# Attention scores from a stacked high-and-low split of queries and keys in place of one fp32 product

## What is computed

```python
def forgetting_attention(q, k, v, f_logit, b_f):
    log_f = jax.nn.log_sigmoid(f_logit.astype(jnp.float32) + b_f.astype(jnp.float32))
    F = jnp.cumsum(log_f, axis=1).transpose(0, 2, 1)
    ...
    def block(args):
        qi, Fi, i = args
        q_pos = i * Q_BLOCK + jnp.arange(Q_BLOCK)
        logits = jnp.einsum('bhqd,bhkd->bhqk', qi, k).astype(jnp.float32) * scale
        logits = logits + (Fi[..., :, None] - F[..., None, :])
        logits = jnp.where(q_pos[:, None] >= k_pos[None, :], logits, -jnp.inf)
        p = jax.nn.softmax(logits, axis=-1)
        return jnp.einsum('bhqk,bhkd->bhqd', p.astype(v.dtype), v)
    ...
```

## Time and profile before

| | |
|---|---|
| median of 3 runs | 2919.59 us |
| lowest, highest | 2916.76, 2920.18 us |
| profiled execution, span | 2917.4 us |
| TensorE busy | 2802.4 us (96%) |
| TensorE weight loads | 2225.7 us (76%) |
| DVE busy | 1768.7 us (61%) |
| ACT busy | 1035.1 us (35%) |
| POOL busy | 26.2 us (1%) |
| mean granted TensorE clock | 0.980 |
| attention stage | about 470.6 to 757 us |

### The profile page before, as it was taken

How to read it: one execution, slowest core, us unless ns; L and a number is a source line. 1 busy time by engine, 2 the same in 40 slices (tenths; PEclk the granted TensorE clock), 3 DMA queues, 4 the chain that set the end, 5 groups by cost and what they waited for, 6 DMA issues and landing times.

```text
span 2917.4 us, 35290 instructions
## 1 busy us (share of the span) xinstructions
PE 2802.4 (96%) x12481; PEld 2225.7 (76%) x12481; DVE 1768.7 (61%) x2713; ACT 1035.1 (35%) x1629; POOL 26.2 (1%) x44
## 2 busy tenths in 40 slices
PE   6999999999999999999999999999999899999996
PEld 3468887777788866788877778787788688888885
DVE  6855675555588757444465747473967776335444
ACT  3032222444332355432243534443422622234224
POOL 0000000000000000000000000000000000000000
PEclk9999999999999989999999999999999999999998
DMA  9966552222356646465522222234566365332331
GB/s 346 350 208 223 187 180 89 73 75 78 128 191 214 223 142 232 156 211 196 183 78 89 89 80 96 72 93 167 198 223 219 101 215 187 98 94 98 127 123 58
DMA packets 240190, 451.26 MB, mean 155 GB/s; under 512 B 23849, under 2 KB 45819, under 8 KB 235437
## 3 DMA queue, kind: packets, MB, share of 16 engines
q1 hardware_dynamic: 237236, 440.80, 45.7%
q0 software_dynamic: 2304, 8.39, 0.8%
q10 hardware_dynamic: 504, 0.17, 0.0%
HBM read 422.01 MB, written 27.30 MB: 154 GB/s over the span
## 4 chain that ended last, share of the span: by engine, by line
PE 74%; issue 13%; DVE 5%; ACT 3%; DVEq 2%; DMA 1%; ACTq 1%; SPq 1%; POOLq 0%; POOL 0%
PE ps L1311 18%; PE ps L1314 18%; PE ps L1317 18%; PE ps L1536 3%; PE ps L1764 2%; PE ps L1324 1%; PE ps L1330 1%; PE ps L1327 1%; PE ps L1268 1%; PE ps L1281 1%; PE ps L1795 1%; PE ps L1798 1%; PE ps L1286 1%; PE ps L1283 1%; PE ps L1681 1%
## 5 line engine op out<-in xcount | busy, mean ns | idle before, releaser
L1311 PE MATMUL ps<-op_hi,w_hi 128*128 128x512 f32 (+2 forms) x2800 | 783.9, 399 | 21.1 <-ACT op_hi L919 7.5
L1821 DVE TENSOR_TENSOR w_lo<-w_raw,w_hi 128x512 fp32r<-128x512 f32 (+2 forms) x672 | 440.9, 662 | 598.0 <-ACT w_hi L681 330.0
L1317 PE MATMUL ps<-op_hi,w_lo 128*128 128x512 f32 (+2 forms) x2800 | 757.1, 390 | 4.0 <-DVE w_lo L1821 4.0
L1314 PE MATMUL ps<-op_lo,w_hi 128*128 128x512 f32 (+2 forms) x2800 | 760.3, 391 | 0.0
L1311 PEld LDWEIGHTS ps<-op_hi,w_hi 128*128 128x128 f32 (+1 forms) x2800 | 520.7, 190 | 140.6 <-issue 26.0
L1317 PEld LDWEIGHTS ps<-op_hi,w_lo 128*128 128x128 f32 (+1 forms) x2800 | 528.7, 189 | 116.2 <-DVE w_lo L1821 5.2
L1314 PEld LDWEIGHTS ps<-op_lo,w_hi 128*128 128x128 f32 (+1 forms) x2800 | 530.0, 189 | 112.8 <-issue 0.3
L681 ACT ACTIVATE w_hi<-w_raw 128x512 fp32r<-128x512 f32 (+2 forms) x416 | 242.6, 592 | 619.5 <-PE ps L1317 451.9
L1844 DVE SCALAR_TENSOR_TENSOR acc<-a_raw,vec,acc 128x512 f32<-128x512 f32 x525 | 381.7, 746 | 15.7 <-DMA a_raw<-in_w_ada 12.8
L706 ACT ACTIVATE w_hi<-w_raw 128x512 fp32r<-128x512 f32 x288 | 181.7, 632 | 588.4 <-PE ps L1317 456.2
L2524 DVE TENSOR_TENSOR w_lo<-w_raw,w_hi 128x512 fp32r<-128x512 f32 x128 | 83.6, 686 | 65.1 <-ACT w_hi L1181 59.8
(11 more groups left out here) (274 smaller groups left out, 2456.8 us busy)
## 6 DMA issues: line engine op xcount, KB each, us to landing
a_raw<-in_w_ada SPq DMA_DIRECT2D x216, 512.0 KB, 4.0
w_raw<-in_w_in_e SPq DMA_DIRECT2D x160, 512.0 KB, 4.7
w_raw<-in_w_in SPq DMA_DIRECT2D x96, 512.0 KB, 4.8
arena<-in_w_ada SPq DMA_DIRECT2D x72, 512.0 KB, 6.8
w_raw<-in_w_in_o SPq DMA_DIRECT2D x64, 512.0 KB, 4.4
w_raw<-in_w_out SPq DMA_DIRECT2D x32, 512.0 KB, 4.8
w_raw<-in_w_out_e SPq DMA_DIRECT2D x32, 512.0 KB, 5.0
w_raw<-in_w_out_o SPq DMA_DIRECT2D x32, 512.0 KB, 3.8
```

What stands on the lines that cost most here:

```text
L1311: mm(ps[0:m, bank + j, 0:tok], hi[:, cols], B.op_hi[:, k, 0:tok], start=first, stop=False)
L1314: mm(ps[0:m, bank + j, 0:tok], hi[:, j * P:j * P + m], B.op_lo[:, k, 0:tok], start=False, stop=False)
L1317: last = mm(ps[0:m, bank + j, 0:tok], lo[:, j * P:j * P + m], B.op_hi[:, k, 0:tok], start=False, stop=last_t)
L1821: V.tensor_tensor(B.w_lo[:, c % RING, 0:width], B.w_raw[:, c // 2 % RAW, c % 2, 0:width], B.w_hi[:, c % RING, 0:width].bitcast(f32), ALU.s ...
```

## The change

Queries q and keys k are split into an fp32r high part and a low part (the rest). A buffer `stage` of three tiles of 128 x 512 is made for each head, with two buffers in turn (one in the place of `B.acc`, one in the arena). With own the 64 rows of the head and other the other 64:

- tile ST_Q: own rows the high part of q, other rows its low part
- tile ST_HIGH: the high part of k, in own and other rows alike
- tile ST_LOW: the low part of k, in own and other rows alike

The score is now two fp32r products into one bank, ST_Q by ST_HIGH and ST_Q by ST_LOW: all 128 rows are used, and (q high + q low) by (k high + k low) comes out.

POOL makes the own rows: two copies with a change of type, and one subtraction. ACT copies the high part of k to the other rows (`stage_high`, in the unit of 256 of the head before, ahead of its exponential). DVE makes the low part of q and k in the other rows (`stage_low`, two subtractions, in the unit of 256 of the head before, behind its `w_lo` tile). Head 0 is made before the stage, behind `part_summed`.

```diff
+def stage_low(B, dve, h):
+    dve.wait_ge(B.sem("stage_high"), h + 1)
+    own, other = head_rows(h)
+    q, k = head_source(B, h)
+    for part, x, high in ((ST_Q, q, ST_Q), (ST_LOW, k, ST_HIGH)):
+        last = B.nc.vector.tensor_tensor(B.stage[h % 2][other, part, :], x,
+                                         B.stage[h % 2][own, high, :].bitcast(mybir.dt.float32),
+                                         mybir.AluOpType.subtract)
+    last.then_inc(B.sem("stage_other_low"), 1)
...
 # pool_program
-    pool.wait_ge(sem("mixing"), HEADS_A)
     for h in range(HEADS_B):
-        if h < 2:
-            nc.gpsimd.memset(queries[others, h, :], 0.0)
-        if h >= 2:
+        if h == 0:
+            pool.wait_ge(sem("part_summed"), o)
+        elif h == 1:
+            pool.wait_ge(sem("mixing"), HEADS_A)
+            pool.wait_ge(sem("mixed"), HEADS_A)
+        else:
             pool.wait_ge(sem("scores"), 4 * (h - 1) + 1)
-        nc.gpsimd.tensor_copy(queries[rows, h % 2, :], B.Y[rows, 8 + h // 2, :])
-        nc.gpsimd.drain().then_inc(sem("queries_in"), 1)
+        nc.gpsimd.tensor_copy(stage[own, ST_Q, :], q)
+        nc.gpsimd.tensor_copy(stage[own, ST_HIGH, :], k)
+        nc.gpsimd.drain().then_inc(sem("stage_high"), 1)
+        nc.gpsimd.tensor_tensor(stage[own, ST_LOW, :], k, stage[own, ST_HIGH, :].bitcast(mybir.dt.float32),
+                                mybir.AluOpType.subtract)
+        nc.gpsimd.drain().then_inc(sem("stage_own_low"), 1)
...
 # attention_scalar
+        Act(B.stage[h % 2][other, ST_HIGH, :], k, ACT.Copy).then_inc(sem("stage_other_high"), 1)
...
+        if u % 4 == STAGE_AT and u // 4 + 1 < HEADS_B:
+            stage_high(u // 4 + 1)
...
 # attention_tensor
-            pe.wait_ge(sem("queries_in"), s // 4 + 1)
-            mm(ps[:, 4 + s % 2, 0:P * (b + 1)], at(AT_QST, 2, S)[:, half, b * P:(b + 1) * P],
-               keys[:, pair, 0:P * (b + 1)], start=True, stop=True).then_inc(sem("scores"), 1)
+            if b == 0:
+                pe.wait_ge(sem("stage_other_high"), s // 4 + 1)
+                pe.wait_ge(sem("stage_own_low"), s // 4 + 1)
+                pe.wait_ge(sem("stage_other_low"), s // 4 + 1)
+            queries = B.stage[half][:, ST_Q, b * P:(b + 1) * P]
+            high, low = (B.stage[half][:, k, 0:P * (b + 1)] for k in (ST_HIGH, ST_LOW))
+            mm(ps[:, 4 + s % 2, 0:P * (b + 1)], queries, high, start=True, stop=False)
+            mm(ps[:, 4 + s % 2, 0:P * (b + 1)], queries, low, start=False, stop=True).then_inc(sem("scores"), 1)
...
 # attention_vector, behind low_to(min(u + 3, UNITS + 4)) and ahead of gated
+        if u % 4 == STAGE_AT and u // 4 + 1 < HEADS_B:
+            stage_low(B, dve, u // 4 + 1)
```

More of the change, by code:

```diff
@@ L192 @@
 AT_VA, AT_K, AT_V, AT_WST, AT_BS, AT_F, AT_FQ = 2048, 6144, 10240, 14336, 15360, 16384, 16896
-AT_NEGF, AT_LOGIT, AT_PT, AT_OTOK, AT_QST, AT_KST = 2048, 3072, 4096, 5120, 14336, 15360
+AT_NEGF, AT_LOGIT, AT_PT, AT_OTOK, AT_STAGE = 2048, 3072, 4096, 5120, 14336
+ST_Q, ST_HIGH, ST_LOW = 0, 1, 2
 AT_XRES, AT_SQ, AT_RSTD, AT_SUM, AT_QSUM = 2048, 4096, 8192, 12544, 13568
@@ L225, in __init__ @@
         self.acc = sb("acc", [P, 2, 2, GC])
+        acc_at = nc.sbuf_base - 4 * 4 * GC
         self.const = sb("const", [P, N_CONST])
@@ L233, in __init__ @@
         self.arena = sb("arena", [P, ARENA])
+        arena_at = nc.sbuf_base - 4 * ARENA
+        self.stage = [nc.alloc_sbuf_tensor_at("stage_even", [P, 3, S], f32r, offset=acc_at),
+                      nc.alloc_sbuf_tensor_at("stage_odd", [P, 3, S], f32r, offset=arena_at + 4 * AT_STAGE)]
         self.ps = nc.alloc_psum_tensor("ps", [P, 8, GC], f32)
@@ L587, with head_rows, head_source @@
 LAG = 3
+def head_rows(h):
+    own, other = (slice(DH_B * (x % 2), DH_B * (x % 2 + 1)) for x in (h, h + 1))
+    return own, other
+def head_source(B, h):
+    own, _ = head_rows(h)
+    return B.Y[own, 8 + h // 2, :], B.at(AT_K, 8, S)[own, h // 2, :]
 def pool_program(B, pool):
@@ L601, in pool_program @@
             .then_inc(B.va_in[b % RAW], 16)
-    queries = at(AT_QST, 2, S)
-    pool.wait_ge(sem("mixing"), HEADS_A)
+    o = ordinal(FIRST["ua"])
     for h in range(HEADS_B):
-        rows, others = (slice(DH_B * (x % 2), DH_B * (x % 2 + 1)) for x in (h, h + 1))
-        if h < 2:
-            nc.gpsimd.memset(queries[others, h, :], 0.0)
-        if h >= 2:
-            pool.wait_ge(sem("scores"), 4 * (h - 1) + 1)
-        nc.gpsimd.tensor_copy(queries[rows, h % 2, :], B.Y[rows, 8 + h // 2, :])
-        nc.gpsimd.drain().then_inc(sem("queries_in"), 1)
+        stage = B.stage[h % 2]
+        own, _ = head_rows(h)
+        q, k = head_source(B, h)
[5 more added lines that the diff above has]
+        else:
+            pool.wait_ge(sem("scores"), 4 * (h - 1) + 1)
+        nc.gpsimd.tensor_copy(stage[own, ST_Q, :], q)
[4 more added lines that the diff above has]
+        nc.gpsimd.drain().then_inc(sem("stage_own_low"), 1)
     n = FIRST["wo1"]
@@ L1115, in pair_out, with stage_high @@
         Act(Y[:, 8 + q, :], ps[:, 6, :], ACT.Copy).then_inc(sem("o_taken"), 1)
+    def stage_high(h):
+        if h == 0:
+            act.wait_ge(sem("part_summed"), ordinal(FIRST["ua"]))
+        elif h == 1:
+            act.wait_ge(sem("mixing"), HEADS_A)
+            act.wait_ge(sem("mixed"), HEADS_A)
+        else:
+            act.wait_ge(sem("scores"), 4 * (h - 1) + 1)
+        _, other = head_rows(h)
+        _, k = head_source(B, h)
+        Act(B.stage[h % 2][other, ST_HIGH, :], k, ACT.Copy).then_inc(sem("stage_other_high"), 1)
+    stage_high(0)
     for u in range(UNITS + 1):
+        if u % 4 == STAGE_AT and u // 4 + 1 < HEADS_B:
+            stage_high(u // 4 + 1)
         if u < UNITS:
@@ L1643, in attention_tensor @@
     mm = nc.tensor.matmul
[L1644 removed]
+    v = at(AT_V, NT, 1024)
     logit, p_t, o_tok = at(AT_LOGIT, 2, S), at(AT_PT, 2, S), at(AT_OTOK, 2, NT, P)
@@ L1668, in attention_tensor @@
         if s < UNITS:
-            pair, half, b = s // 8, s // 4 % 2, s % 4
+            half, b = s // 4 % 2, s % 4
             pe.wait_ge(sem("score_slots"), s + 1)
-            pe.wait_ge(sem("queries_in"), s // 4 + 1)
-            mm(ps[:, 4 + s % 2, 0:P * (b + 1)], at(AT_QST, 2, S)[:, half, b * P:(b + 1) * P],
-               keys[:, pair, 0:P * (b + 1)], start=True, stop=True).then_inc(sem("scores"), 1)
+            if b == 0:
[6 more added lines that the diff above has]
+            mm(ps[:, 4 + s % 2, 0:P * (b + 1)], queries, low, start=False, stop=True).then_inc(sem("scores"), 1)
         if s >= 2:
@@ L2351, in vector_program @@
             take_part(g["part"], ps[:, 7, :], ordinal(n + 1))
+            stage_low(B, dve, 0)
             dve.wait_ge(sem("bs_in"), 16)
```

2 lines of the change are left out of this document (added).

## The result

| | before | after |
|---|---|---|
| median | 2919.89 us (2916.76 to 2920.27, 4 runs) | 2944.53 us (2941.92 to 2952.08, 4 runs) |
| profiled execution, span | 2917.4 us | 2945.0 us |
| first to last logits of the attention | 273.83 us | 296.39 us |

The changed kernel is slower: the ratio is 1.0089, with a 95% interval of 1.0075 to 1.0104. The direction was forecast, but the time lies 10.5 us above the 2934 us and just outside the range. Of the 27.6 us between the two profiled executions, 22.6 lie in the attention.

What follows compares the result with a forecast made beforehand. The chain of DVE and ACT was taken to bound the kernel. Subtractions net of gains (+0.2 us) and POOL beside DVE (+14.6) made +14.8; with 2917.4 and 2.2 to the median this gave 2934 us, range 2914 to 2944.

Steps and rivals of the forecast that it cites:

- Part 5: POOL's copies and subtraction beside DVE's low part and mask around units of 512: 1.0 us in 14 heads, +14.6 us.
- Part 2: DVE's two subtractions, behind the low part on the chain: 1.3 us in each of 15 heads, all units' sum +0.2 us.
- What bounds the kernel: Attention: a chain of DVE and ACT from logits to logits takes 14.66 of a head's 16.32 us; TensorE adds 1.66 at most.
- Part 1: Score products on TensorE: the fp32r pair takes 0.46 us at 512 columns instead of 0.86, saving 14.2 us for 16 heads.
- rivals C and D: C: TensorE's 14.2 us all show, 2905 us, chance 0.14. D: the fp32r pair is no shorter, 2924 us, chance 0.06.
- Part 3: ACT's copy of the keys' high part, about 0.6 us a head, hidden ahead of an exponential that waits for DVE.
- Part 4: Staging of head 0 while TensorE mixes, with a row ISA ahead of POOL's first subtraction: 0 us.
- rival B: DVE and POOL exclude each other while both read SBUF: +14.8 us, 2934 us, 2926 to 2943, chance 0.48.
- The upper end of Part 5: POOL beside DVE, with POOL's subtraction twice as long as a copy: 1.6 us a head, +23 us.

Runs made afterwards that it cites:

- experiment 1: Changed kernel with POOL's two copies and subtraction replaced by memsets of the same tiles, which read nothing: 2923.63 us, ratio 1.0016.
- experiment 5: Kernel before with its fp32 score product replaced by two fp32r products of tiles that lie ready, no staging on DVE or ACT: 2911.70 us, ratio 0.9981.
- Experiment 4: Kernel before with two unread DVE subtractions of 64 x 512 added behind the low part in each unit of 256: 2925.76 us, ratio 1.0014.
- Experiments 1 to 3: Changed kernel with POOL's work as memsets (2923.63 us), with POOL starting behind the mask of 512 (2926.57 us), with only POOL's subtraction as memsets (2927.46 us).

## Why the prediction was right and wrong

| step | forecast | measured |
|---|---|---|
| Part 5, POOL beside DVE | +14.6 | about +12.8 |
| Part 2, 11 units of 256 | +2.9 | +4.6 |
| Part 2, gating | +3.9 | +4.0 |
| Part 2, units of 384 without a meeting (3.80 in experiment 1) | -2.3 | -2.3 |
| Part 2, units of 128 (without unit 12) | -3.4 | -3.2 |
| Part 2, first and last head | -0.9 | -0.7 |
| the clock of TensorE | no term | +7.4 |
| sum in the stage | +14.8 | +22.6 |

- **What bounds the kernel** held: in heads 1 to 14 no logits of 384 or 128 wait for scores, and experiment 5 found the chain's floors of 3.80 and 4.28 us.
- **Part 1** held to 0.01 us in the rows; rivals C and D are out.
- **Part 2** was right in its mechanism and short in its size. The pair costs 1.44 us, not 1.3: the 0.61 us from one instruction to the next hold between the two subtractions, but the first one starts 0.73 behind the low part's start, and the logits 0.71 behind the second. Unit 5 took 5.12 us, and 5.12 and 5.10 in experiments 1 and 4. Experiment 4, without the new products, has the same 4.74 and 7.27 us.
- **Part 3** held: ACT's exponential waits for the maximum (3.84 us idle in the row at 619.41).
- **Part 4** held: the first logits stand at 475.24 against 474.26, 1.0 us later, and the mixing products of the earlier trace rows started 1.35 us later already (459.98). The row ISA is within 0.53 us in which POOL does nothing.
- **Part 5**, rival B, held in kind, and came near in sum by luck. It gave 0.5 us to the low part and 0.5 to the mask, in 14 heads. (14 times 1.0 is 14.0; the sum has 14.6.) The low part loses 0.22, since POOL's first copy is 0.24 us ahead of it and not level with it (the lead is 1.07 us, not 0.74). The mask loses 1.06, since it meets the subtraction of 1.29 us, which I had entered with a copy's 0.61, but it does so in nine heads and not in 14. In the three gating heads the trace before could have told: there POOL's copy begins 2.02 us ahead of the logits of 512 (552.08 against 554.10), and not 0.03 behind them. The upper end of Part 5, a subtraction twice as long as a copy, had the right length; it gives 2943 us, which the range does not leave out, other than the text says. The Trainium skill, GPSIMD Engine Reference (3.1), has POOL's addition of two tensors at 1.96 times DVE's time; the subtraction here takes 1.29 us against 0.69.
- **The failed step** is one that isn't in the sum. It let TensorE's idle time grow, by 21 us in the stage, and gave that idle time no price. In the products of a weight tile the clock at its lower level costs 0.20 us each (0.43 against 0.23). It fell in units 12, 16, 32 and 48 (+5.0 us) and in the turns of heads 4, 8 and 12 (+2.4). Experiments 1 to 3, without the long mask, have 6.2 to 7.0 us in units 16, 32 and 48, so part of the 20.9 us of experiment 1 is this term. Between the forecast sum of the stage and the measured one, the 7.4 us of the clock and 1.7 of the units of 256 are offset by 1.8 too much in Part 5; 0.5 us are smaller rows. With 2 us outside the stage and 0.7 between the sum and the stated 2934 us this is the 10.5 us. Without the clock's term the time would have come out at about 2937 us, an estimate from 2944.5 - 7.4.

## What to carry to other kernels

Ask of each engine in order what chain runs through it, and where in that chain it idles. Work that a change adds there costs nothing ahead of the wait and its full time behind it: the same two subtractions cost 7.3 us of the stage behind the low part (1.7 of them by the clock) and are hidden ahead of it. And where GpSimd and VectorE both read SBUF, a short VectorE instruction on the chain pays the length of the GpSimd one that it comes behind, so let GpSimd start from an event at which VectorE begins to wait, not from TensorE's progress. And idle time that a change gives to TensorE is not free: here its clock fell in seven units, which cost 7.4 us.

## What the hardware showed beyond what was expected

- The meeting is not a slowdown but a turn-taking: a mask of 0.29 us took 1.35 beside a subtraction of 1.29, and ended 0.15 us behind it. POOL's memsets, which read nothing, cost DVE nothing (0.69 and 0.29 us beside them).
- POOL waits as well: its second copy took 1.08 us behind DVE's low part instead of 0.61.
- Logits, which read one tile of SBUF and the scores, met the copies in each head and took 0.73 to 0.75 us, as without them.
- TensorE's granted clock fell in unit 32 during the second of two waits, of 1.64 and 1.19 us, and in unit 19 behind one of 2.51 us. With 1.75 us of products in place of the first wait it did not fall in unit 32, although the second was still there.
